# A two-layer hybrid encoder in one kernel: 48 output-projection products moved into the last attention head, and a new order of work where the MLP begins

## The reference, cut to what matters

```
# 1024 tokens, width 1024, all float32; layer 0 (mixer A), then layer 1 (mixer B)
h = rms_norm(x, attn_norm_g[0])
# 8 heads; each: two softmaxes of q.k + ALiBi, chunk-causal; w = p0 - lam*p1; o = w @ v
o = rms_norm(o, subln_g) * (1 - lambda_init)       # per head
x = x + o.reshape(s, 1024) @ w_o                   # output projection
x = x + square(relu(rms_norm(x, mlp_norm_g) @ w_up)) @ w_down     # width 4096
# shared k, v from x; layer 1: windowed attention with sinks, its own w_o; a second MLP
```

## Time and profile before

| | us |
|---|---|
| median of 3 runs | 2190.8 (2190.15 to 2192.13) |
| the profiled execution | 2187.25 |
| its span in the trace | 2184.8 |
| PE busy | 2138.0 (98%) |
| DVE busy | 1548.9 (71%) |
| ACT busy | 1139.0 (52%) |
| POOL busy | 711.0 (33%) |

### The profile page before, as it was taken

How to read it: one execution, slowest core, us unless ns; L and a number is a source line. 1 busy time by engine, 2 the same in 40 slices (tenths; PEclk the granted TensorE clock), 3 DMA queues, 4 the chain that set the end, 5 groups by cost and what they waited for, 6 DMA issues and landing times.

```text
span 2184.8 us, 34712 instructions
## 1 busy us (share of the span) xinstructions
PE 2138.0 (98%) x11580; PEld 1838.6 (84%) x11580; DVE 1548.9 (71%) x3023; ACT 1139.0 (52%) x2431; POOL 711.0 (33%) x1182
## 2 busy tenths in 40 slices
PE   7999999988999999999999999999999999999999
PEld 7899999977888888878888899988888888788887
DVE  6788788786586666777767757775766666876783
ACT  6566666655455455624434447664555555444342
POOL 4333433331642222132134225445622222112221
PEclk9999999999999999999999999999999999999999
DMA  7111110003424444744544111105244445754352
GB/s 220 30 30 30 30 29 23 1 21 111 130 87 159 159 155 139 280 174 168 184 139 159 63 53 49 30 11 174 92 159 159 150 139 209 260 193 147 104 188 82
DMA packets 191205, 257.72 MB, mean 118 GB/s; under 512 B 15168, under 2 KB 139584, under 8 KB 186432
## 3 DMA queue, kind: packets, MB, share of 16 engines
q1 hardware_dynamic: 191040, 255.65, 35.2%
HBM read 174.09 MB, written 79.69 MB: 116 GB/s over the span
## 4 chain that ended last, share of the span: by engine, by line
PE 77%; issue 9%; DVE 7%; POOLq 3%; ACT 1%; POOL 1%; DMA 1%; DVEq 0%; ACTq 0%; SPq 0%
PE score L2277 43%; PE trb L2277 15%; PE proj L2277 11%; PE pv L2277 5%; DVE xop L1609 2%; DVE xT L1935 1%; POOLq L536 1%; POOLq L538 1%; DVE w_op L1609 1%; POOL qk L905 1%; PE trb L2324 1%; DMA xop<-u_dram 1%; POOLq L534 1%; POOLq L530 1%; PE trb L2735 0%
## 5 line engine op out<-in xcount | busy, mean ns | idle before, releaser
L2277 PE MATMUL score<-xop,w_op 128*128 128x512 f32 x3840 | 889.1, 391 | 6.0 <-issue 3.3
L2277 PEld LDWEIGHTS score<-xop,w_op 128*128 128x128 f32 x3840 | 721.2, 188 | 159.2 <-issue 9.0
L2277 PE MATMUL trb<-xop,w_op 128*128 128x512 f32 x1536 | 361.9, 390 | 3.7 <-DVE xop L1609 3.7
L930 POOL TENSOR_TENSOR w_quad<-w_quad,w_sum 128x512 f32<-128x512 f32 x56 | 73.3, 1308 | 841.0 <-DVE w_op L1609 841.0
L2277 PEld LDWEIGHTS trb<-xop,w_op 128*128 128x128 f32 x1536 | 287.4, 188 | 67.0 <-issue 7.8
L1075 ACT ACTIVATE w_op<-w_quad 128x512 fp32r<-128x512 f32 (+1 forms) x336 | 212.6, 643 | 214.7 <-PE score L2277 93.2
L1609 DVE TENSOR_TENSOR w_op<-w_quad,w_op 128x512 fp32r<-128x512 f32 (+1 forms) x335 | 280.2, 840 | 41.3 <-ACT w_op L1075 41.3
L1935 DVE TENSOR_TENSOR xT<-score,xT 128x512 f32<-128x512 f32 x160 | 109.1, 686 | 145.1 <-PE score L2277 139.2
L1075 ACT ACTIVATE xop<-xop 128x1024 fp32r<-128x1024 f32 x112 | 117.2, 1054 | 61.6 <-DMA xop<-u_dram 61.3
L1075 ACT ACTIVATE quad<-score 128x512 f32<-128x512 f32 x96 | 57.3, 596 | 176.6 <-PE score L2277 174.2
L1180 ACT ACTIVATE p<-p,nm_a,slopes 128x128 f32<-128x128 f32 (+7 forms) x112 | 96.4, 863 | 90.2 <-DVE nm_a L1807 90.2
(11 more groups left out here) (331 smaller groups left out, 4298.7 us busy)
## 6 DMA issues: line engine op xcount, KB each, us to landing
xop<-u_dram SPq DMA_DIRECT2D x112, 512.0 KB, 5.4
u_dram<-quad SPq DMA_DIRECT2D x30, 1536.0 KB, 9.6
w_quad<-in_mlp_w_up SPq DMA_DIRECT2D x64, 512.0 KB, 5.5
w_quad<-in_mlp_w_down SPq DMA_DIRECT2D x64, 512.0 KB, 5.0
wa_raw<-in_a_w_qkv SPq DMA_DIRECT2D x96, 128.0 KB, 2.4
u_dram<-quad SPq DMA_DIRECT2D x34, 256.0 KB, 3.9
quad<-xT_dram SPq DMA_DIRECT2D x32, 256.0 KB, 3.7
xT_dram<-xs SPq DMA_DIRECT2D x32, 256.0 KB, 2.3
```

The costliest lines, as they stand in the source:

```text
L930: return pool.tensor_tensor(out, x, y, ALU.subtract)
L2277: return nc.tensor.matmul(out, a, b, start=start, stop=stop, **kw)
```

## The change

Three things are changed.

- **The last head of layer 0 gets 48 panel products.** They are high products of chunks 0 to 5: 12 each of panel 0's second half, panel 2's first half and panel 2's second half, accumulated one after the other in `proj`, copied by ACT to SBUF (`kept`) and later added by POOL to the x that `add_x` reads; and 12 of panel 0's first half, which stay in `proj`. Panel 0 is loaded and split in head 6 (its low part by DVE there), panel 2's low part is made by POOL, panel 1 is split in the last head. `a_hi` of chunks 0 to 5 is made at the head's start, `o_factors` comes one block earlier. Panels 4 to 7 and their splits get other places.
- **The first MLP operands come in another order** on DVE, ACT and POOL, in both segments.
- **The sums of squares** are two blocks each behind the four groups of three products of step 4, not all eight behind step 3; the squares of panel 6 go to another tile and are added later.

```
+LATE = 6
+SPLIT_ORDER = (0, 2, 1, 3, 4, 5, 6, 7)
+KEPT = ((0, 1), (2, 0), (2, 1))
+FIRST_PLACES = (2, 1, 0, None, 1, 2, 0, 1)
-        wo_bank = [[bank[0], bank[1], [proj[:, :], pv[:, :]]],
+        wo_bank = [[[proj[:, :], pv[:, :]], bank[1], bank[0]],
 # SP
+            sp.wait_ge(wa_lo_done, NH * 4)
+            sp.dma_start(w_raw2, w_out[0]...[:, :, 0:P]).then_inc(w_in[0], 16)
 # POOL, after its last norm of q and k
+            def last_head():
+                pool.wait_ge(w_hi_done, split_count(0, 2))
+                for k in range(0, KC, 2):
+                    last = pool.tensor_tensor(w_lo[0][:, k:k + 2, :], w_raw[0][:, k:k + 2, :], w_hi[0]..., ALU.subtract)
+                norm_outputs(NH - 1, head_out[0])
+                    pool.wait_ge(half_steps, 2)
+                    pool.wait_ge(quad_in[0], 64)
+                    pool.tensor_tensor(x, x, kept[0][:, :], ALU.add).then_inc(half_added, 1)
 # POOL, start of the MLP
-                    if c < KC - 1:
+                    if c < KC - 2:
                         for half in range(2):
-                            add_square(square_of(c, half), half, 36 * seg + 2 * c + half + 1)
+                            add_square(panel_square(c, half), half, 36 * seg + 2 * c + half + 1)
+                    elif i == 0:
+                        first_sum("S2")
...
                         if c == KC - 1:
+                            first_sum("S3")
...
+                for half in range(2):
+                    add_square(panel_square(KC - 2, half), half, 36 * seg + 2 * KC - 4 + half + 1)
 # ACT
+                def keep(i):
+                    act.wait_ge(half_steps, 2 * i + 1)
+                    copy(kept[i][:, :], proj[:, :]).then_inc(half_steps, 1)
                 def squares(i):
-                    if i == KC - 1:
-                        act.wait_ge(panel_half, 2 * KC * (seg + 1))
+                    if i >= KC - 2:
+                        act.wait_ge(panel_half, 2 * KC * (seg + 1) - (KC - 1 - i))
 # DVE, start of the MLP
-                for k in range(4):
-                    op_of_weights(k)
+                op_of_weights(0)
                 add_x(KC - 1, (1,))
-                for slot in range(2):
+                for slot in range(3):
                     for u in (2, 3):
                         unit_lo(u, slot)
-                add_x(KC - 1, (0,))
+                    if slot == 1:
+                        add_x(KC - 1, (0,))
+                    op_of_weights(slot + 1)
 # DVE, last head
-                    if s == NB - 1:
-                        split_panel(0)
                     mix(h, s, par, s % 2)
 # PE
+            def panel_high(out, panel, half, chunks):
+                for c in chunks:
+                    pe.wait_ge(o_early_hi, c + 1)
+                    mm(out, w_h[:, c, :], x_h, c == 0 or kept_half and c == LATE, False)
+                    last = mm(out, w_l[:, c, :], x_h, False, kept_half and c == LATE - 1)
 # PE, head 7, after the transposes of block s, ahead of scores and values
+                    if s == 0:
+                        panel_high(proj[:, :], 0, 1, (3,))
+                    if s == 2:
+                        panel_high(proj[:, :], 0, 1, (4, 5)).then_inc(half_steps, 1)
+                    if s == 3:
+                        pe.wait_ge(half_steps, 2)
+                        pe.wait_ge(w_lo_done, split_count(0, 2))
+                        panel_high(proj[:, :], 2, 0, (0, 1, 2))
+                    if s == 4:
+                        panel_high(proj[:, :], 2, 0, (3, 4, 5)).then_inc(half_steps, 1)
...
-                    if k == 3:
-                        sum_squares()
+                        if k == 4:
+                            sum_squares(range(2 * kp, 2 * kp + 2))
```

More of the change, by code:

```diff
@@ L240, in trunk @@
         scope = ExitStack()
+        kept = [sb(f"kept{i}", [P, HALF], F32, scope) for i in range(3)]
+        scope.close()
+        scope = ExitStack()
         x_tok = [sb("x_tok0", [P, 4, D], F32, scope)]
@@ L339, in panel_parts, with splits_ahead, split_count @@
         def panel_parts(seg, i):
-            return w_first if seg and i == 0 else (w_hi[i % 3], w_lo[i % 3])
+            if i == 3 and not seg:
+                return w_op[:, 4, :, :].rearrange("p a (k n) -> p (a k) n", n=P), w_low3[:, :, :]
+            if seg and i == 0:
+                return w_first
+            place = i % 3 if seg else FIRST_PLACES[i]
+            return w_hi[place], w_lo[place]
+        def splits_ahead(seg, i):
+            return ((i + 2,) if i + 2 < KC else ()) if seg else {1: (4,), 4: (6,), 5: (7,)}.get(i, ())
+        def split_count(seg, panel):
+            return KC * seg + (panel if seg else SPLIT_ORDER.index(panel)) + 1
         oT = xT
@@ L936, in segment @@
                 clear()
+                if seg == 0:
+                    pool.wait_ge(half_steps, 6)
+                    pool.wait_ge(quad_in[1], 64)
+                    for half in range(2):
+                        x = quad[1][:, TILE[0, half], :]
+                        pool.tensor_tensor(x, x, kept[1 + half][:, :], ALU.add).then_inc(half_added, 1)
                 def sum_weights(n, part):
@@ L1403, in segment @@
                         unit_hi(u, slot)
+                    if slot == 0:
+                        scaled(KC - 1, (1,))
+                    if slot < 2:
+                        op_of_weights(slot + 1)
                 scaled(KC - 1, (0,))
+                for k in range(3, 5):
+                    op_of_weights(k)
                 def x_bank(n):
@@ L1954, in add_x @@
                         dve.wait_ge(quad_in[u % 2], 64 * (2 * seg + u // 2 + 1))
+                        if seg == 0 and (i, half) in KEPT:
+                            dve.wait_ge(half_added, KEPT.index((i, half)) + 1)
                         if i:
@@ L2489, in head, with panel_lows @@
                         values(uses, s, (s - 1) % NB, h * 4 + (s - 1) // 2, par if s else 1 - par)
+            def panel_high(out, panel, half, chunks):
+                for c in chunks:
+                    pe.wait_ge(o_early_hi, c + 1)
+                    x_h = a_hi[:, c, HALF * half:HALF * (half + 1)]
+                    kept_half = (panel, half) in KEPT
+                    w_h, w_l = panel_parts(0, panel)
+                    mm(out, w_h[:, c, :], x_h, c == 0 or kept_half and c == LATE, False)
+                    last = mm(out, w_l[:, c, :], x_h, False, kept_half and c == LATE - 1)
+                return last
+            def panel_lows(panel, chunks):
+                for c in chunks:
+                    pe.wait_ge(o_split, c + 1)
+                    for half in range(2):
+                        mm(wo_bank[0][panel][half], panel_parts(0, panel)[0][:, c, :], a_lo[:, c, HALF * half:HALF * (half + 1)], False, False)
             def panel_products(seg, panel, x_hi, x_lo, k):
```

222 lines of the change are left out of this document (147 added, 75 removed).

## The result

The changed kernel is slower: 2203.78 us median against 2190.48 for before on the same chip (6 runs each), ratio 1.0056, 95% interval 1.0043 to 1.0069. The forecast was 2184.5, its range 2175 to 2189.5. The profiled execution, the fastest of the six of the changed kernel, took 2199.7 us, span 2197.2, so 12.4 more than the span of before, and a ledger of starts on PE says where. All numbers but the right column are starts or distances on PE's timeline.

A forecast was written before the change was run, and what follows sets the result against it. PE, busy 2138.0 of 2184.8 us, was taken as the bound from attention's end to the MLP, DVE's queue at the MLP start. -12.3 + 6.0 = -6.3 us gave 2180.95 profiled, 2184.5 as median; range 2175 to 2189.5.

The forecast's parts named there:

- Part 1: 48 products moved from the panels into the last head: -10.9 us there and -1.4 in the head, -12.3.
- part 2: New operand order and moved sums of squares at both MLP starts: 2 x 3.0 = +6.0 us.
- Both signs of being wrong: Last head longer than 50 us; at the MLP start, spread following step 7 without a wait, or DVE's operations taking 0.6.
- Moving the sums can gain nothing by itself: MLP start: PE's lost 1.84 us was already covered by DVE's queue; only a shorter queue would gain.
- 3.0 + 1.9: MLP start, upper bound for one layer: +4.9 us if PE's clock also falls after the new waits.
- DVE's queue, +3.0 per layer: MLP start: nine of twelve DVE operations run beside POOL at 1.69 us, so the last factor comes 3.0 us later.
- whatever PE need not do there is saved: End of attention to MLP: PE never idles, so removing 48 products of 0.227 us saves 10.9 us.
- Panels run without idle time: Panels: later add_x of panels 1 and 2 costs nothing, needed only 10.9 and 21.8 us after panel 2's end.
- The last head, -1.4: Last head: by a walk at full clock, block 7's values end at 513.8, not 515.2; range -2.5 to +4.
- The mix is on the chain: Last head: DVE loses panel 0's split of 1.22 us ahead of the last mix, gaining about 1.1 us.
- 1.00 wherever PE is busy throughout: Argument against the slower case: new products fill gaps in the last head, and fewer gaps mean a higher clock.
- My slower rival: PE stays at 1.2 GHz through the last head and is its bound there: 2200.9 us, chance 0.06.

The follow-up runs named there:

- between_alone: Kernel before, with only the sums of squares moved between the groups of step 4: 2196.07 us, ratio 1.0031.
- part2_alone: Kernel before, with both MLP starts (operand order and sums of squares) as in the changed kernel: 2207.03 us, ratio 1.0074.
- order_behind: Kernel before, with the new operand order in both MLP starts but all sums of squares behind step 3 as before: 2196.57 us, ratio 1.0030.
- fill_gap: part2_alone with 12 useless 512-column matmuls ahead of step 4 of each MLP start: 2197.16 us, ratio 1.0028.
- part1_alone: Changed kernel with both MLP starts as before, leaving the last head and panels changed: 2191.84 us, ratio 1.0003.
- less48: Kernel before, with the 48 high products done nowhere and the last head's output transposes behind chunk 6: ratios 0.9971 and 0.9983.
- panels_in_time: part1_alone with panel 4 loaded right behind panel 3 and panels 4 and 5 split one panel later in the order: 2187.47 us, ratio 0.9988.
- stores_first: panels_in_time with panel 0's stores issued ahead of the loads of unit 1 and the first MLP weights: 2186.25 us, ratio 0.9982.
- squares6_early: part2_alone with panel 6's squares added by POOL at their old place and in their old tile: 2196.98 us, ratio 1.0030.

## Why the prediction was wrong

Both parts of the sum failed. Part 1 was put at -12.3 and measures +0.7 alone; part 2 was put at +6.0 and measures +16.2 alone. Both signs of being wrong came: the last head is longer than 50 us (50.68), and in layer 1 the spread follows step 7 without a wait.

**Part 2, the step that failed: "Moving the sums can gain nothing by itself", taken to cost nothing either.** The sums of squares took 1.84 us on PE and I counted them as work. They were also cover: PE could not have started step 4 much earlier, since the bank copy was not done. In the trace of before it ends at 616.08, and PE starts at 616.18:

```profile
615.50 0.58 ACT L1075 ACTIVATE quad<-score 128x512 f32<-128x512 f32 x1
```

The 0.22 us of "issue" behind the sums was the visible end of that wait. Moved away, they leave 1.9 us of idle time in the old order and 3.13 in the new. The cost is 6.8 to 9.6 us for two layers (between_alone; part2_alone against order_behind), 8.3 in the changed kernel. It is the clock: at 1.00 behind the gap the same edit costs 0.2 us in a layer, at 0.50 it costs 5.0 (between_alone), and filling the gap gives back 10 (fill_gap).

**The clock.** I took the low clock of before as covered by DVE's queue and bounded a layer by 3.0 + 1.9. In layer 1 PE at half clock comes to the spread 4.4 us after DVE's last factor: the bound changed hands. I had written that PE would wait 2 us for the factors.

**DVE's queue, +3.0 per layer: the mechanism was right.** Alone (order_behind) it measured 3.3. In the trace of the changed kernel the last factor of layer 1 ends 29.64 us after the first MLP step, where it ended after 25.61 in layer 0 of before, so +4.0. Count and price were right: 3 x 0.60 + 9 x 1.69 = 17.0 us were forecast for the twelve operations, and they take 17.02 (1559.42 to 1576.44). What was missed is mainly their start, 4.19 us after the first step and not 3.3; the pair ahead of them, at 1555.42, stands beside POOL too and takes 3.48 us. The waits were forecast as 1 us at step 3 (1.05 ahead of step 2 and 0.63 within step 3 in layer 1) and 1 at step 4 (3.13); at step 4 I had asked for the weights and not for the bank. A pair of operations costs 1.69, as in the rows, and not 1.90; the exclusive lock of which the Trainium skill speaks ("SBUF — State Buffer", section "SBUF: two separate sides") gives the direction, and the row the size.

**Part 1, -10.9: "whatever PE need not do there is saved".** PE's stretch did shrink, by 8.14, and by 6.9 in part1_alone. But its 88.0 us at full busy share did not say how far behind the next chain was. In part1_alone the first MLP start of layer 0 gives 8.1 back. In less48, where the 48 products are done nowhere, 3.7 to 6.4 us are left of the 10.9, part of the loss being of the edit's own making.

**"Panels run without idle time", covered by panels 3 and 4: failed.** I asked which PE work needs `add_x` of panels 1 and 2 (a bank, 10.9 and 21.8 us later). But unit 0's operands, the loads of units 2 and 3 into its tiles and so the first MLP step need it too, without such slack. panels_in_time puts 3.3 us to it, and stores_first 1.3 more. What holds the rest of the wait (4.49 us in stores_first) stays open.

**The last head, -1.4: +1.95, inside the range of -2.5 to +4.** The end was right (products over the wait, 1.0 given back). Two steps of the walk were not. "The mix is on the chain": DVE does come to the last mix 1.1 us earlier, counted from the start of the values of block 6 (0.33 us behind it and not 1.47). But the transposes stand behind these values in PE's queue, and already before the change they followed them without a wait (510.45 in the earlier trace rows has no bracket). In the changed kernel the values of block 6 begin 41.84 us after the start of the head, where it was 40.86. The other step is the full clock: it fell to 0.50 again, by 479.51, when the new wait had not yet come. Before that PE has waited 0.97 and 0.83 us for DVE, at places where it had waited before the change as well. The rival's "1.00 wherever PE is busy throughout" does not hold in its own rows either: the earlier trace rows has 10.00 us busy of 10 at 0.83. The low part that POOL makes beside `o_factors` I had priced at nothing; what it costs the head is not shown.

**Right:** head 6 costs nothing (468.11 against 466.47 is the first load but for 0.1), and the transposes do not wait for the normalised output.

**The parts do not add up.** Part 1 alone is +0.7, part 2 alone +16, both +12: in layer 0 the new order waits less for the operands that part 1 makes late (0.74, 0.73 and 0.72 us over the first two steps and 1.96 ahead of the third, where the old order waits 1.03 and 6.63 in the first). My slower rival had a chance of 0.06 and another mechanism. It was the half-clock idea applied to the wrong place. The measured time lies beyond its 2200.9, but not by its mechanism: the last head grew by 1.95 us and not by 15.

## What to carry to other kernels

Before work is moved out of a gap's neighbourhood, ask what wait it covers: small instructions ahead of a short "issue" gap may be all that keeps the engine busy while a bank is emptied. Where PE is busy throughout, leave the work out altogether once and time it, before building its move, and see in the trace which waits the leaving out makes by itself. And for a step that comes late, follow every user to the next stage, not only the one on the busy engine.

## What the runs showed of the hardware that was not expected

- After the same idle time PE's clock may fall or stay. In between_alone PE idles 1.90 us ahead of step 4 in both layers, behind the same 24 products; layer 0 goes on at 0.50, layer 1 at 1.00:

```profile
620.00:625.00 5.00, 5.00 (x18) 4.33 (x18) 5.00 (x6) 0.63 (x1) 2.30 (x2) 0.50 0.00 0
...
1575.00:1580.00 5.00, 5.00 (x25) 4.19 (x25) 5.00 (x9) 2.34 (x5) 0.30 (x1) 1.00 0.06 15
```

  In squares6_early, with 1.87 and 1.86 us, it is the other way round. Its times scatter with it: 11.6 us between the fastest and the slowest of 8 runs, against 5.6 in 26 runs of before on the same chip. Why the clock falls once and stays once is not shown.
- VectorE's smallest instructions suffer from GpSimd too. Of the five of `o_factors` (8 columns) four take 0.17 to 0.24 us alone and 0.53 to 0.62 beside it, and one takes 0.16 in both; a subtraction of two tiles of 512 columns takes 1.7 in place of 0.60.
- Two stores of 256 KB issued behind ten other transfers landed 8.4 us after VectorE could have used the buffer (panels_in_time). Issued ahead of six of them (stores_first), the next `add_x` waited 1.41 us for ScalarE and 0.16 for them.
